# The mixer's steps in one order for all engines, its decay exponents summed in PSUM, and GpSimd forming its low weight parts

## The reference, cut to what matters

```python
p = h @ w_in                                  # 1024 -> 2576 columns
oa = rms_norm(diff_attend(q, k, v, lam)) ...  # 4 heads, softmax minus lam * softmax
ob = window_attend(q, k, v, sink)             # 4 query heads on 2 key heads
z, xs, B, C, dt = conv_silu(p)                # SSD: 8 heads of 64, two directions
y[l] = sum_s (C_l . B_s) * exp(cs_l - cs_s) * dt_s * x_s   (s <= l in its chunk of 128)
     + exp(cs_l) * (C_l . state)
oc = rms_norm((y + d_skip * xs) * silu(z))
x = x + gate * (concat(oa, ob, oc) @ w_out)
```

## Time and profile before

| | |
|---|---|
| median of 3 runs | 2050.27 us (2048.05 to 2052.09) |
| the profiled execution | 2050.99 us |
| its span, first to last instruction | 2049.2 us |
| TensorE busy | 1802.8 us (88%) |
| VectorE busy | 1465.1 us (71%) |
| ScalarE busy | 716.3 us (35%) |
| GpSimd busy | 94.0 us (5%) |
| granted TensorE clock, mean | 0.946 |

### The profile page before, as it was taken

One profiled execution on the slowest core, in us unless ns is written; L12 is line 12 of the kernel. 1 busy time (PEld: TensorE's weight loads), 2 busy tenths in 40 slices (PEclk: granted clock), 3 DMA queues, 4 the chain that ended last, 5 costly groups with the idle time before them and its releaser, 6 DMA issues. The chain is left out here.

```text
span 2049.2 us, 25282 instructions
## 1 busy us (share of the span) xinstructions
PE 1802.8 (88%) x8940; PEld 1472.6 (72%) x8940; DVE 1465.1 (71%) x2465; ACT 716.3 (35%) x1043; POOL 94.0 (5%) x159
## 2 busy tenths in 40 slices
PE   0799999979956898999999979999997984788999
PEld 0588888857734456788888768888885773478999
DVE  7987878777577844978787767787856756746666
ACT  3422122244434544421222252222225433545342
POOL 0000000000022000000000000000000003000000
PEclk9999999989977988999999999999998986899999
DMA  8545444404233004454444414444421324134552
GB/s 316 189 166 183 150 157 164 164 21 136 104 81 64 1 22 184 165 184 145 162 164 162 166 62 144 167 144 181 143 84 43 128 103 69 14 124 144 184 184 103
DMA packets 39917, 269.97 MB, mean 132 GB/s; under 512 B 5104, under 2 KB 6448, under 8 KB 9136
## 3 DMA queue, kind: packets, MB, share of 16 engines
q1 hardware_dynamic: 25776, 183.28, 24.9%
q0 software_dynamic: 14080, 85.89, 13.0%
HBM read 262.99 MB, written 5.37 MB: 131 GB/s over the span
## 5 line engine op out<-in xcount | busy, mean ns | idle before, releaser
L1253 PE MATMUL ps<-h_hi,w_hi 128*128 128x512 f32 (+1 forms) x1872 | 690.0, 369 | 70.5 <-DVE h_lo L832 70.5
L1254 PE MATMUL ps<-h_lo,w_hi 128*128 128x512 f32 (+1 forms) x1872 | 684.4, 366 | 0.0
L1255 PE MATMUL ps<-h_hi,w_lo 128*128 128x512 f32 (+1 forms) x1872 | 683.9, 365 | 0.0
L1253 PEld LDWEIGHTS ps<-h_hi,w_hi 128*128 128x128 f32 x1872 | 357.2, 191 | 139.3 <-issue 69.1
L763 DVE TENSOR_TENSOR w_lo<-raw,w_hi 128x2048 fp32r<-128x2048 f32 (+1 forms) x162 | 366.4, 2262 | 97.4 <-ACT w_hi L470 97.3
L861 DVE SCALAR_TENSOR_TENSOR x_res<-ps,abg,x_res 128x256 f32<-128x256 f32 x640 | 272.0, 477 | 204.8 <-PE ps L1255 186.2
L470 ACT ACTIVATE w_hi<-raw 128x2048 fp32r<-128x2048 f32 (+1 forms) x162 | 306.3, 1891 | 279.2 <-PE ps L1255 275.3
L1254 PEld LDWEIGHTS ps<-h_lo,w_hi 128*128 128x128 f32 x1872 | 356.9, 191 | 57.7 <-issue 1.2
L1255 PEld LDWEIGHTS ps<-h_hi,w_lo 128*128 128x128 f32 x1872 | 356.4, 190 | 57.6
L780 DVE CUSTOM_DVE_ANT_0 mod_prod<-mod_raw,cb 128x1024 f32<-128x1024 f32 x288 | 338.3, 1218 | 14.8 <-DMA mod_raw<-mod_in 13.3
L1253 PE MATMUL ps<-a_hi,w_hi 128*128 128x512 f32 (+1 forms) x704 | 258.1, 367 | 15.6 <-DVE a_lo L855 13.4
(11 more groups left out here) (162 smaller groups left out, 1266.5 us busy)
## 6 DMA issues: line engine op xcount, KB each, us to landing
raw<-ffn_in SPq DMA_DIRECT2D x132, 1024.0 KB, 4.9
mod_raw<-mod_in POOLq DMA_DIRECT2D x72, 1024.0 KB, 5.1
raw<-proj_in SPq DMA_DIRECT2D x20, 1024.0 KB, 5.6
raw<-out_w_in SPq DMA_DIRECT2D x8, 1024.0 KB, 4.8
x_spill<-x_res SPq DMA_DIRECT2D x2, 2048.0 KB, 7.3
eo<-decay_rows POOLq DMA_DIRECT2D x8, 512.0 KB, 5.5
x_res<-x_spill SPq DMA_DIRECT2D x2, 2048.0 KB, 8.9
cb<-c_in SPq DMA_DIRECT2D x2, 1024.0 KB, 9.5
```

The lines of the kernel that those rows point to most:

```text
L1253: pe.matmul(dst, w_hi[:, slot, wsl], hi, start=first, stop=False)
L1254: pe.matmul(dst, w_hi[:, slot, wsl], lo, start=False, stop=False)
L1255: return pe.matmul(dst, w_lo[:, slot, wsl], hi, start=False, stop=last)
```

## The change

The changed kernel replaces `STEPS`, the calls after it and the planned asides with one list for each layer that all engines walk, GpSimd too.

- `PROJECT` works by tiles rather than units. The dt unit comes first and its 16 columns are multiplied in turn with the first convolution tile. The states (x, s, r) and the heads (hx, hm, hc, hy, hg) stand between the tiles of the projection. The last two tiles (19 and 20, of z) stand in the attention.
- The exponents of a pair are summed in a PSUM bank by TensorE: an identity times a triangle of 0 and -2^100, a selector times the rows, and 128-column products of the rows with the selector. ScalarE takes the exponential from PSUM; the subtraction and minimum on VectorE, the DRAM rows and the broadcasts are gone, and `cb` is no longer masked. The rows carry a high and a low part. For `cexp` TensorE broadcasts a row into PSUM in plain float32 (hc) and VectorE multiplies. Matrices lie in a ring of six.
- VectorE keeps the low parts of the mixer's units 0 to 2; GpSimd forms those of units 3 to 14 (12 a layer).
- The mixer's loads use two slots of `raw` instead of three; the third of the FFN is another buffer. The FFN after the mixer waits for the low part of unit 14 before it loads any of its own.
- In the attention an item needs its own scores, its weights come before the next item's maximum on VectorE, transposes use bank 6 alone and values bank 7 alone; the maxima come negated, so that one small VectorE operation goes for each item. Parts of output tiles 0 to 3 (Os, Oa, 18 of 24 matmuls each) stand between the items. The z gate's SiLU moves there as well (zs), with its table loads.
- `x_res` comes back when the heads are done.

The core of the diff:

```diff
+    k[:, K_TRI:K_TRI + P] = np.where(i[None, :] >= i[:, None], 0.0, DROP)
+    k[:, K_TRI + P:K_TRI + 2 * P] = np.where(i[None, :] <= i[:, None], 0.0, DROP)
...
+        PROJECT = [("T0", 0), ("E", 0), ("R", 0), ("E", 1), ("R", 1), ("S", 0),
+                   ("T", 2), ("E", 2), ("cv", 0), ("R", 2), ("S", 1),
+                   ("T", 3), ("cv", 1), ("R", 3), ("si", 0), ("E", 3),
+                   ("T", 4), ("cv", 2), ("si", 1), ("E", 4), ("S", 2),
+                   ("T", 5), ("cv", 3), ("si", 2), ("E", 5),
+                   ("T", 6), ("cv", 4), ("si", 3), ("E", 6), ("S", 3),
+                   ("T", 7), ("cv", 5), ("si", 4), ("E", 7),
+                   ("T", 8), ("si", 5), ("E", 8), ("t", 0), ("t", 1), ("t", 2), ("t", 3), ("S", 4),
+                   ("T", 9), ("b", 0), ("E", 9), ("t", 4), ("t", 5), ("t", 6), ("t", 7),
+                   ("T", 10), ("b", 1), ("E", 10), ("c", 0), ("x", 0), ("S", 5),
+                   ("T", 11), ("s", 0), ("b", 2), ("E", 11), ("c", 1), ("r", 0), ("x", 1),
+                   ("T", 12), ("s", 1), ("b", 3), ("E", 12), ("hx", 0), ("hx", 1), ("c", 2), ("r", 1), ("x", 2), ("S", 6),
+                   ("T", 13), ("v", 0), ("E", 13), ("s", 2), ("hx", 2), ("hx", 3), ("c", 3), ("hm", 0), ("hm", 1), ("r", 2),
+                   ("T", 14), ("v", 1), ("E", 14), ("hc", 0), ("hc", 1), ("hm", 2), ("hm", 3), ("hx", 4), ("hx", 5), ("S", 7),
+                   ("T", 15), ("hy", 0), ("b", 4), ("E", 15), ("hm", 4), ("hm", 5), ("hg", 0), ("hx", 6), ("hx", 7), ("c", 4),
+                   ("T", 16), ("b", 5), ("E", 16), ("hc", 2), ("hc", 3), ("hm", 6), ("hm", 7), ("hx", 8), ("hx", 9), ("c", 5), ("S", 8),
+                   ("T", 17), ("hy", 1), ("v", 2), ("b", 6), ("hm", 8), ("hm", 9), ("hg", 1), ("hx", 10), ("hx", 11), ("c", 6),
+                   ("hc", 4), ("hc", 5), ("hm", 10), ("hm", 11), ("hx", 12), ("hx", 13),
+                   ("T", 18), ("hy", 2), ("hm", 12), ("hm", 13), ("hg", 2), ("hc", 6), ("hc", 7), ("hx", 14), ("hx", 15),
+                   ("hm", 14), ("hm", 15), ("S", 9)]
...
+        BESIDE = {0: {0: [("Ta", 19)], 1: [("Tb", 19), ("E", 19)], 2: [("Ta", 20)], 3: [("Tb", 20), ("E", 20)], 4: [("zs", 0), ("S", 10)],
+                      5: [("g", 0), ("g", 1)], 6: [("g", 2), ("g", 3), ("sq", 0), ("me", 0)], 7: [("sq", 1), ("me", 1), ("ro", 0)],
+                      8: [("no", 0), ("ro", 1)], 9: [("no", 1), ("hi", 0), ("ot", 0)], 10: [("lo", 0), ("hi", 1)], 11: [("lo", 1), ("sq", 2)],
+                      12: [("Os", 0)], 14: [("Os", 1)], 17: [("ot", 1), ("sq", 3)], 18: [("me", 2), ("me", 3)], 19: [("ro", 2), ("ro", 3)],
+                      20: [("no", 2), ("no", 3), ("Os", 2)], 21: [("hi", 2), ("hi", 3)], 22: [("lo", 2), ("lo", 3), ("Os", 3)],
+                      24: [("Oa", 0)], 25: [("ot", 2)], 26: [("Oa", 1), ("hi", 4)], 27: [("lo", 4)], 28: [("Oa", 2)], 30: [("Oa", 3)],
+                      33: [("ot", 3), ("hi", 5), ("lo", 5)]},
+                  1: {0: [("T", 19), ("E", 19)], 1: [("T", 20), ("E", 20)], 2: [("zs", 0), ("S", 10)], 3: [("g", 0), ("g", 1), ("g", 2), ("g", 3)],
+                      4: [("sq", 0), ("me", 0)], 5: [("ot", 0), ("sq", 1), ("me", 1), ("ro", 0)], 6: [("no", 0), ("ro", 1), ("hi", 0)],
+                      7: [("no", 1), ("lo", 0), ("hi", 1), ("sq", 2)], 8: [("lo", 1)], 9: [("Os", 0), ("ot", 1), ("sq", 3)],
+                      10: [("me", 2), ("me", 3), ("Os", 1), ("ro", 2), ("ro", 3)], 11: [("no", 2), ("no", 3), ("hi", 2), ("hi", 3), ("Os", 2)],
+                      12: [("lo", 2), ("lo", 3), ("Os", 3)], 13: [("ot", 2), ("Oa", 0)], 14: [("hi", 4), ("Oa", 1)], 15: [("lo", 4), ("Oa", 2)],
+                      16: [("Oa", 3)], 17: [("ot", 3), ("hi", 5), ("lo", 5)]}}
...
+            n = len(att_items(layer))
+            order = PROJECT + [("hy", 3), ("hg", 3), ("E", 17), ("E", 18)]
+            for i in range(n + 2):
+                front = [("sc", i), ("wt", i - 1), ("mx", i), ("pv", i - 2)]
+                back = [("tr", i - 1), ("ex", i), ("ev", i - 1)]
+                order = (order + [s for s in front if 0 <= s[1] < n] + BESIDE[layer].get(i, [])
+                         + [s for s in back if 0 <= s[1] < n])
+            return order
...
+                    sp.wait_ge(lo_ready, base - 2 if m == 0 else base - 1 if m == 1 else base + m - 1)
...
-                        load(out_w_in[layer, m - PROJ_UNITS], u % 3, u // 3)
+                        sp.dma_start(raw[:, m % 2, :], out_w_in[layer, m - PROJ_UNITS]).then_inc(mix_in[m % 2], 16)
+                    if m == PROJ_UNITS + 1:
+
+                        sp.wait_ge(hd_mm, 4 * (layer + 1))
+                        sp.wait_ge(spilled, 16 * (layer + 1))
+                        sp.dma_start(x_res[:, :, :].rearrange("p k t -> p (k t)"), spill).then_inc(x_back, 16)
...
+                for kind, j in steps(layer) + [("S", PROJ_UNITS)]:
+                    if kind == "S":
+                        m = j + 3
+                        pool.wait_ge(hi_ready, mix_base(layer) + m + 1)
+                        if m == 3:
+                            pool.wait_ge(lo_ready, mix_base(layer) + 3)
+                        pool.tensor_tensor(w_lo[:, m % 3, :], raw[:, m % 2, :], w_hi[:, m % 3, :], ALU.subtract).then_inc(lo_ready, 1)
...
+                    elif kind == "hx":
+                        act.wait_ge(x_mm, DECAYS * layer + j + 1)
+                        if j >= RING:
+                            act.wait_ge(hd_mm, 4 * layer + (j - RING) // 4 + 1)
+                        act.activation(m_t[:, j % RING, 0:nt], ps[:, 4 + j % 2, 0:nt], ACT.Exp).then_inc(ex_done, 1)
+                    elif kind == "zs":
+                        for i in range(4):
+                            act.wait_ge(pj_evac, NT * layer + TILE_AT["z", i] + 1)
+                            act.activation(zs[:, i, 0:nt], zs[:, i, 0:nt], ACT.Silu).then_inc(z_silu, 1)
+                        table_ln_exp()
...
+            def split_mix(layer, m):
+                if m >= 3:
+                    return
+                n = P if m == DT_UNIT else UNIT
+                dve.wait_ge(hi_ready, mix_base(layer) + m + 1)
+                tt(w_lo[:, m % 3, 0:n], raw[:, m % 2, 0:n], w_hi[:, m % 3, 0:n], ALU.subtract).then_inc(lo_ready, 1)
+
+            def split_next(layer, m):
+                if m < MIX_UNITS:
+                    split_mix(layer, m)
+                else:
+                    if m == MIX_UNITS:
+                        dve.wait_ge(lo_ready, mix_base(layer) + MIX_UNITS)
+                    split(m - MIX_UNITS, 2 * layer + 1, 0)
...
-                    for c in range(nt // P):
-                        x = ts(dd[:, h % 4, d, c * P:(c + 1) * P], eo[:, h % 2, d, c * P:(c + 1) * P],
-                               dcol[:, c, 8 * d + h:8 * d + h + 1], 0.0, ALU.subtract, ALU.min)
-                    x.then_inc(d_done, 1)
...
+                if what == "hm":
+                    dve.wait_ge(ex_done, DECAYS * layer + i + 1)
+                    m = m_t[:, i % RING, 0:nt]
+                    tt(m, m, cbt[:, i // 8, 0:nt // P, :].rearrange("p c t -> p (c t)"), ALU.mult).then_inc(mt_done, 1)
+                elif what == "hc":
+                    dve.wait_ge(ce_mm, HEADS * layer + i + 1)
+                    if i == 0:
+                        dve.wait_ge(c_two_in, 64 * (layer + 1))
+                    if i >= 2:
+                        dve.wait_ge(hd_mm, 4 * layer + i // 2)
+                    tt(cexp[:, i % 2, 0:nt], c_two[:, i // 4, 0:nt], ps[:, 7, 0:nt], ALU.mult).then_inc(cexp_done, 1)
...
+                    pick = sel_r[:, r:r + 1].to_broadcast([P, P])
...
+                    bank = 4 + i % 2
+                    pe.matmul(ps[:, bank, 0:nt].rearrange("p (c t) -> p c t", c=nct), ident_r[:, :],
+                              drop_r[:, d, :].unsqueeze(1).to_broadcast([P, nct, P]), start=True, stop=False)
+                    pe.matmul(ps[:, bank, 0:nt], pick, e_rows[:, 0:nt], start=False, stop=False)
+                    for c in range(nct):
+                        last = pe.matmul(ps[:, bank, c * P:(c + 1) * P], g_rows[:, c * P:(c + 1) * P], pick,
+                                         start=False, stop=c == nct - 1)
+                    last.then_inc(x_mm, 1)
+                elif what == "hc":
...
+                        pe.wait_ge(st_done, 6 * (layer + 1))
+                    for d in range(2):
+                        last = pe.matmul(ps[64 * d:64 * d + 64, 7, 0:nt], sel_r[:, 8 * d + i:8 * d + i + 1].bitcast(F32).to_broadcast([P, 64]),
+                                         x_rows[:, 0:nt].bitcast(F32), start=True, stop=True)
...
+                ks = {"Os": [4, 5, 6, 7], "Oa": [0, 1], "Ob": [2, 3], "Of": [4, 5, 6, 7, 0, 1, 2, 3]}[part]
+                if part == "Os":
+                    split_ready(u % 3, u // 3)
+                    pe.wait_ge(mix_lo_s, 8 * layer + 4)
+                    pe.wait_ge(frst, 2 * (4 * layer + m) + 2)
+                elif part == "Oa":
```

(16 more changed lines are left out.)

1197 lines of the change are left out of this document (592 added, 605 removed), and 5 rows, old and new, of the table STEPS.

## The result

The changed kernel took 2109.82 us (2107.99 to 2114.11, 4 runs) against 2051.18 for the kernel before, a ratio of 1.0264 with an interval of 1.0218 to 1.0311. It is some 58 us slower; I had said 2045.9 and a range of 1990 to 2085, so it lies outside the range, on the slow side. The profiled execution has a span of 2107.4 us against 2049.2.

What follows compares the result with a forecast made beforehand. TensorE, busy 88% of the span, was taken as the bound, with the two SSD stages (119.7 us) all there was to win. Projection/SSD -32.2, attention A +39.0, B +5.9, output -22.1, FFN +5 gave -4.4: 2045.9 us, range 1990 to 2085.

Steps and rivals of the forecast that it cites:

- GpSimd terms: GpSimd's low parts blocking VectorE: 8 us a layer in projection and SSD, 3 us a layer in attention A.
- Part 2: GpSimd's low parts: 4.57 us each, blocking VectorE 0 to 46 us per layer on the path, taken as 8.
- Rival 2: Slower: GpSimd blocks VectorE where TensorE waits for it, 22.9 us per layer against 8; about 2076 us; chance 0.30.
- Part 1: Projection and SSD in one order: TensorE's work sets most, old waits stay; with GpSimd's blocking, -16.1 us in each layer.
- Rival 1: TensorE has no more to wait for: old waits of 17.3 and 29.0 us are filled; about 2000 us; chance 0.28.
- The start, +10.3,: Each mixer's start: TensorE waits for the second unit's low part before its first tile, +10.3 us per layer.
- Stage A: Attention A: weights before the next maximum, so nothing overlaps; 72.3 against 51.4 and 44.3 against 26.2 us, +20.9 and +18.1.
- The chain's sum: Attention A's serial maximum, exponentials and weights: 4.74 us an item with 512 keys, 3.37 with 256; 64.9 us in layer 0.
- the gate's block and the split: Beside attention A's items: SiLU with table loads and rounding, 4.4 and 3.4 us, and a GpSimd split, 3 us.
- Layer 0's B: Attention B, layer 0: 48 output matmuls add 10.9 us, a higher clock offsets them; change 0, bounds -2 and +7.
- Layer 1, +5.9,: Attention B, layer 1: clock already 1.0, so output matmuls moved in make it 38.6 against 32.7 us, +5.9.
- part 5, +5,: The FFN behind the mixer: its loads wait for GpSimd's last split; bounds 0 to 13.6 us, taken as +5.

## Why the prediction was wrong, by its steps

**No single step made the miss of 64 us.** With GpSimd's low parts taken off, the mixers were still 24 us longer than before, where the forecast without its GpSimd terms (8 and 3 us a layer, 22 in all) is -26.4: 50 us of miss are left. The other 14 are GpSimd's: 36 measured, 22 forecast. Each of the next two steps would have turned the sign of -4.4 by itself.

**Part 2, "I take under two splits' worth, 8 us per layer", failed.** The effect was seen in the earlier trace rows, its bounds (0 to 46 us per layer in part 1) were right, and I chose near the lower end, by VectorE's mean idle share. Taking GpSimd's low parts off shortened a mixer by 17.7 and 18.4 us although VectorE then had 27 us more work, and doubling GpSimd's work added 43.8 and 42.3 us. Rival 2 had the right mechanism, and its 22.9 us per layer are nearer than 8; the 18 us are net of what VectorE's own low parts cost on the path, which no run shows. Its time of 2076 is not what came, since it knew nothing of the other 50 us. A mean share was the wrong row. The splits stand in the order where VectorE's SBUF-to-SBUF work does, in the convolutions and the state products, and it is there that TensorE waits for VectorE.

The page "SBUF — State Buffer" of the Trainium skill (section "SBUF: two separate sides") told which operations stop: with two SBUF inputs as well as fast modes. The trace agrees: `xdec` and the row at 528.72 waited, the row at 528.06 with a PSUM operand did not. I had read it as support for rival 2 and did not move the term.

**Part 1, the old waits "I keep these", 17.3 and 29.0 us, failed, and has the largest share.** After the start the forecast without its 8 us for GpSimd was 172.5 us in layer 0 and 150.7 in layer 1; with GpSimd out of it 189.8 and 158.5 were measured, 17 and 8 us more. It is waiting rather than work: TensorE's busy time was 168.9 us in layer 0, 10 above both stages before, where I had 6 more. The waits shown for that run make up 19.2 of its 20.8 idle us, and 12.3 of them are hand-overs: for `cexp` 7.2 and for the rotated tile 5.1. Pulling them apart shortened part 1 by 6 us in layer 0 and 4 in layer 1, most of which stage A took back. Rival 1 (no more waits) was wrong: the woven order has new ones. That single buffers make them is argued, not shown; no run has a second bank there.

**The start, +10.3,** was measured as +10.4, but ought not to stand in the sum at its full size: the other engines began 25.4 us after the mean in either kernel, and undoing the late start gave back 2.4 and 1.6 us. So the +10.4 was compensated in part 1.

**Stage A.** The chain's sum was right to 2% (64.9 against 66.4 us without the gate's block), by errors that cancel: items with 512 keys took 4.4 us for 4.74, and those with 256 took 3.0 where nothing held them and 3.9 on average for 3.37. The rest was sized too low, the gate's block and the split: 4.4 + 3 us beside the chain (the first term's own numbers give 4.3), where 81.9 - 66.4 = 15.5 were measured. I had left out that ScalarE's exponentials stand in order behind evacuations that wait for TensorE's tile; putting these later gave 6.8 us with GpSimd's low parts and 1.6 without. Later I expected the old order to undo the loss, and in all three runs with it it did not: it removes the wait for exponentials, and VectorE waits for TensorE's scores instead.

**Stage B and output.** Layer 0's B, "0 (bounds -2 and +7)", took +6.1: the clock rose from 0.82 to 0.97 as I had assumed, and TensorE's busy time from 52.7 to 57.7 us. I had 55. Layer 1, +5.9, took +11.0, with a clock of 0.93 for my 1.0. The output stages came within 2 us. The FFN's part 5, +5, was 10.3 - 4.2 = 6.1 in layer 1 and nothing in layer 0, between the last output product and the mean.

What stays open: why B slows by 6 to 8 us under the old order, and how much of stage A's loss the clock explains (0.79, before 0.87), since waiting and a low clock go together. No run holds the clock fixed. Nor does a run give the transposes and values their two banks each again, a rival for stage A that is untested.

## What to carry to other kernels

A helper whose operations stop the engine that supplies the bottleneck is not free: count the operations of both that read SBUF in the same stretch, and price a block at the full length of the helper's operation wherever a product is waited for. In an order that all engines walk, an item's time is the longest in-order path through its neighbours; what is put between two items must wait for nothing itself. And undo parts one by one before trusting a sum: of seven edits that were to help, one helped clearly, two came out 5 and 7 us lower and two 8 and 11 us higher with intervals that overlap, and two made it clearly worse.

## What the runs showed that I had not expected

- Blocked time counts as VectorE's busy time: 117.1 us with GpSimd's help, 115.4 with ten more 2.29 us operations of its own.
- Doubling GpSimd's work cost 0.7 us per us (76 of 110), at a GpSimd share of 8% of the span in the changed kernel.
- A multiplication by a column in the rows' chain on 16 partitions took 4.78 us beside a low part, where its neighbour took 0.41: it was held as long as an operation on 128 partitions (4.85).
- Stages that no edit touched differed by 4 to 5 us between the profiled executions of the variants.
